# Hybrid HGRN2 / latent-attention / SwiGLU layer: tokens handed over column by column, the first weight block as an array of its own, token sums loaded one by one

## The reference

```
h    = rms_norm(x, attn_norm_w)
proj = h @ w_in                        # 2048 x 5184: hq hf hi hg (1024 each), c_q 512, c_kv 512, k_r 64
o_a  = hgrn2_mixer(hq, hf, hi, hg)     # gated linear recurrence in chunks of 64
o_b  = mla_mixer(c_q, c_kv, k_r)       # low-rank attention, RMS norms on the latents and on each head
x    = x + concat(o_a, o_b) @ w_out
h    = rms_norm(x, ffn_norm_w)
x    = x + (silu(gate) * up) @ w_down  # gate, up = h @ w_gate_up, D_FF = 5632
```

## Time and profile before

| | |
|---|---|
| median of 3 runs | 1115.05 us (1113.57 to 1115.18) |
| the profiled execution | 1115.01 us |
| its span, first to last instruction | 1113.3 us |
| PE busy | 1103.5 us (99%) |
| DVE / ACT / POOL busy | 900.2 / 644.7 / 61.0 us |
| DMA | 230.01 MB, mean 207 GB/s |
| chain that ended last | PE 91%, DVE 4%, DMA 2% |

### The profile page before, as it was taken

One profiled execution on the slowest core, in us unless ns is written; L12 is line 12 of the kernel. 1 busy time (PEld: TensorE's weight loads), 2 busy tenths in 40 slices (PEclk: granted clock), 3 DMA queues, 4 the chain that ended last, 5 costly groups with the idle time before them and its releaser, 6 DMA issues.

```text
span 1113.3 us, 15363 instructions
## 1 busy us (share of the span) xinstructions
PE 1103.5 (99%) x5176; PEld 927.6 (83%) x5176; DVE 900.2 (81%) x1234; ACT 644.7 (58%) x910; POOL 61.0 (5%) x154
## 2 busy tenths in 40 slices
PE   8999999999999999999999999999999999999998
PEld 7988888888888888888888888888888878888887
DVE  6688787587876577588988888988988889999887
ACT  7566777668654466365455555554554555655553
POOL 4200000000000000000000000000000020000000
PEclk9999999999999999999999999999999999999999
DMA  8766455554655455767777777787777786666665
GB/s 269 209 187 200 146 169 157 157 162 152 230 183 172 164 176 171 227 218 224 234 236 225 228 233 220 230 240 218 233 237 228 233 290 210 200 215 202 197 205 170
DMA packets 107557, 230.01 MB, mean 207 GB/s; under 512 B 8265, under 2 KB 19314, under 8 KB 107250
## 3 DMA queue, kind: packets, MB, share of 16 engines
q1 hardware_dynamic: 101346, 209.30, 60.3%
q0 software_dynamic: 5856, 19.93, 5.7%
q10 hardware_dynamic: 304, 0.14, 0.0%
HBM read 218.85 MB, written 10.49 MB: 206 GB/s over the span
## 4 chain that ended last, share of the span: by engine, by line
PE 91%; DVE 4%; DMA 2%; ACT 1%; issue 1%; SPq 0%; DVEq 0%; ACTq 0%
PE side L1975 22%; PE main L1731 20%; PE side L1977 11%; PE main L1734 10%; PE side L1945 4%; PE side L1946 4%; PE side L1947 4%; PE main L1945 3%; PE main L1946 3%; PE main L1947 3%; DMA raw<-in_w_down 1%; PE main L1751 1%; PE side L1773 1%; DVE w_lo L1122 1%; PE side L1870 1%
## 5 line engine op out<-in xcount | busy, mean ns | idle before, releaser
L1013 ACT CAST w_hi<-raw 128x1024 fp32r<-128x1024 f32 x245 | 239.8, 984 | 162.8 <-PE side L1975 62.8
L1573 DVE TENSOR_TENSOR w_lo<-raw,w_hi 128x1024 fp32r<-128x1024 f32 x245 | 274.6, 1133 | 17.7 <-ACT w_hi L1013 17.5
L1122 DVE TENSOR_TENSOR w_lo<-raw,w_hi 128x1024 fp32r<-128x1024 f32 (+3 forms) x156 | 178.8, 1156 | 97.1 <-ACT w_hi L793 94.4
L793 ACT CAST w_hi<-raw 128x1024 fp32r<-128x1024 f32 (+3 forms) x156 | 153.4, 993 | 130.2 <-PE main L1731 125.4
L1731 PE MATMUL main<-w_hi,hT_hi 128*128 128x512 f32 (+2 forms) x416 | 161.2, 388 | 0.2 <-issue 0.2
L1734 PE MATMUL main<-w_hi,hT_lo 128*128 128x512 f32 (+2 forms) x416 | 157.6, 380 | 0.0
L1975 PE MATMUL side<-w_hi,hT_hi 128*128 128x512 f32 x400 | 155.6, 389 | 0.0
L1977 PE MATMUL side<-w_hi,hT_lo 128*128 128x512 f32 x400 | 155.6, 389 | 0.0
L1731 PE MATMUL main<-w_lo,hT_hi 128*128 128x512 f32 (+2 forms) x416 | 107.1, 379 | 0.0
L1975 PE MATMUL side<-w_lo,hT_hi 128*128 128x512 f32 x400 | 106.9, 389 | 0.0
L1731 PEld LDWEIGHTS main<-w_hi,hT_hi 128*128 128x128 f32 x416 | 78.2, 188 | 13.2 <-issue 0.4
(11 more groups left out here) (292 smaller groups left out, 1887.5 us busy)
## 6 DMA issues: line engine op xcount, KB each, us to landing
raw<-in_w_gate_up SPq DMA_DIRECT2D x176, 512.0 KB, 4.8
raw<-in_w_down SPq DMA_DIRECT2D x88, 512.0 KB, 4.5
raw<-in_w_in SPq DMA_DIRECT2D x64, 512.0 KB, 4.0
raw<-in_w_out SPq DMA_DIRECT2D x32, 512.0 KB, 3.6
raw<-in_w_in SPq DMA_DIRECT2D x15, 384.0 KB, 5.0
squares<-hiddenT POOLq DMA_DIRECT2D x11, 512.0 KB, 5.3
hiddenT<-squares POOLq DMA_DIRECT2D x44, 128.0 KB, 5.2
raw<-in_w_ukv SPq DMA_DIRECT2D x8, 512.0 KB, 4.0
```

The lines of the kernel that those rows point to most:

```text
L793: copy(w_hi[:, slot, 0:n], raw[:, slot, 0:n]).then_inc(s_hi, 1)
L1013: copy(w_hi[:, n % RING, 0:cols], src).then_inc(s_hi, 1)
L1122: tt(w_lo[:, slot, 0:n], raw[:, slot, 0:n], w_hi[:, slot, 0:n].bitcast(F32), ALU.subtract)\
L1573: tt(w_lo[:, n % RING, 0:cols], src, w_hi[:, n % RING, 0:cols].bitcast(F32), ALU.subtract)\
```

## The change

- **x with columns on partitions.** The host hands over a second copy of x, `columns`: per partition p the 41 norm weights that belong to it, then 16 tiles of 256 tokens. The loads (`load_tokens`, nine of them) put it into `x_columns`, which lies over the memory of `hT_lo`; ACT rounds it from there into `hT_hi`, DVE writes `hT_lo` over it in place. The transposes of x and of the norm weights are gone from PE, and `vec_cols` is the start of `x_columns`, filled by the first load.
- **The first block's weights** are a contiguous array of their own, `w_first` (2048 x 384). Its first granule is loaded from ACT's queue, the others from SP's.
- **x itself** (tokens on partitions) is still needed for the squares and is loaded later, in four loads of 512 KB behind the loads of granules 11, 12, 14 and 16. `sq1` moves to positions 10, 12, 13 and 15, `r1a` and `r1b` to 16 and 17.
- **r_in** is no longer there when block 0's products are read: `lat_in` copies them unscaled, `lat_a` scales inside the square, and `lat_b` multiplies by both factors. `k_r` is still scaled in `lat_in`.
- **POOL's wait** is now for the last of these four loads; the three small loads that are left come behind granules 18 to 20.
- **Token sums** are asked for one product at a time, when PE has used 0, 0, 4, 8, 13, 19, 25, 31, 37 and 43 granules of w_down.

The core of the diff:

```
+SUMS_FROM = (0, 0, 4, 8, 13, 19, 25, 31, 37, 43)
-X_AFTER = {1: (2,), 2: (3,), 3: (4,), 4: (5,), 5: (6,), 6: (7,), 7: (8,)}
-X_TURNED = (FIRST, -1, 1, 2, 3, 4, 5, 6, 7)
+XT_AFTER = {1: (1,), 2: (2,), 3: (3, 4), 4: (5,), 5: (6,), 6: (7,), 7: (8,)}
+X_AFTER = {11: 0, 12: 1, 14: 2, 16: 3}
+SMALL_AFTER = 18
...
-    s = [(FIRST, ("vec", 0))] + [(at, ("x", p)) for p, at in enumerate(X_TURNED)]
-    s += [(2 * c + 3, ("sq1", c)) for c in range(4)]
-    s += [(10, ("r1a",)), (11, ("r1b",)), (19, ("vec", 1))]
+    s = [(at, ("sq1", c)) for c, at in enumerate((10, 12, 13, 15))]
+    s += [(16, ("r1a",)), (17, ("r1b",))]
...
+        x_columns = sb("x_columns", [P, GAP + KT * SEQ], F32, loaded)[:, GAP - V_ROWS:]
+        loaded.close()
+        sb("vec_cols", [P, GAP])
+        vec_cols = x_columns[:, 0:V_ROWS]
         hT_lo = sb("hT_lo", [P, KT, SEQ], F32R)
...
+        def load_tokens(p):
+            k, wide = PIECES[p]
+            c0, c1 = V_ROWS + SEQ * k if p else 0, V_ROWS + SEQ * (k + wide)
+            nc.sync.dma_start(x_columns[:, c0:c1], columns[:, c0:c1]).then_inc(s_xt[p], 16)
...
-            load_x(sp, 0)
-            for g, (b, k, n) in enumerate(GRANULES):
+            load_tokens(0)
+            for g in range(1, G0):
                 if g >= RING:
                     slot_free(g)
+                load_granule(sp, g)
+                for p in XT_AFTER.get(g, ()):
+                    load_tokens(p)
+                if g in X_AFTER:
+                    cols = slice(NB * X_AFTER[g], NB * (X_AFTER[g] + 1))
+                    sp.dma_start(X[:, :, cols], x_v[:, :, cols]).then_inc(s_x[X_AFTER[g]], 16)
...
-            pool.wait_ge(s_x[len(PIECES) - 1], 16)
+            pool.wait_ge(s_x[3], 16)
             pool.dma_start(lb[:, :, :], hgrn_lb[:, 0:GW].partition_broadcast(P)).then_inc(s_lbin, 16)
...
-                pool.wait_ge(s_used, W1 + 2 * c)
                 for n, p in enumerate(CHUNKS[c]):
+                    pool.wait_ge(s_used, W1 + SUMS_FROM[p])
...
                 elif kind == "sq1":
                     c = a[0]
+                    act.wait_ge(s_x[c], 16)
...
+                    act.wait_ge(s_inv, RMS.index(("r1a",)) + 1)
                     for t in range(NT):
-                        square(latents[i][:, t, :], sumsq[:, t:t + 1])
+                        square(latents[i][:, t, :], sumsq[:, t:t + 1], scale=r_in[:, t:t + 1])
...
-                        ts(v, v, inv[:, t:t + 1], None, ALU.mult).then_inc(s_lat, 1)
+                        ts(v, v, inv[:, t:t + 1], r_in[:, t:t + 1], ALU.mult, ALU.mult).then_inc(s_lat, 1)
...
-            act.dma_start(vec_rows[0:KT, :], attn_norm_w.rearrange("a (k p) -> (a k) p", p=P)).then_inc(s_attn, 16)
-            load_x(act, 1)
+            load_granule(act, 0)
```

More of the change, by code:

```diff
@@ L79, in main_blocks @@
     for n, cols in enumerate(LAT_COLS):
-        w.append(("lat", n, "w_in", at, cols, rows(KT), 2))
+        w.append(("lat", n, "w_in", at, cols, rows(KT), 2) if n else ("lat", n, "w_first", 0, cols, rows(KT), 2))
         at += cols
@@ L274, in schedule @@
     s += [(e + 3, ("r2a",)), (e + 4, ("r2b",))]
+    s += [(at, ("x", p)) for p, at in enumerate(X_SPLIT)]
     return sorted(s, key=lambda x: x[0])
@@ L359, in split_needed, with hybrid_layer @@
     return SPLIT[("x", len(PIECES) - 1)] + 1
-def hybrid_layer(nc, x, positions, attn_norm_w, w_in, hgrn_lb, hgrn_norm_w, mla_q_norm_w, w_uq, mla_kv_norm_w,
-                 w_ukv, q_head_norm_w, k_head_norm_w, w_out, ffn_norm_w, w_gate_up, w_down, out):
-    weights = {"w_in": w_in[0], "w_uq": w_uq[0], "w_ukv": w_ukv[0], "w_out": w_out[0]}
+def hybrid_layer(nc, x, columns, positions, w_first, w_in, hgrn_lb, w_uq, w_ukv, q_head_norm_w, k_head_norm_w, w_out, w_gate_up,
+                 w_down, out):
+    weights = {"w_first": w_first, "w_in": w_in[0], "w_uq": w_uq[0], "w_ukv": w_ukv[0], "w_out": w_out[0]}
     w_gu = w_gate_up[0]
@@ L494, in hybrid_layer @@
         s_tlo = sem("s_tlo")
-        s_x = [sem(f"s_x{p}") for p in range(len(PIECES))]
-        s_attn = sem("s_attn")
+        s_xt = [sem(f"s_xt{p}") for p in range(len(PIECES))]
+        s_x = [sem(f"s_x{c}") for c in range(4)]
         s_small = sem("s_small")
@@ L844, in step @@
                 kind, a = s[0], s[1:]
[L845 to L851, removed]
+                if kind == "x":
+                    k, wide = PIECES[a[0]]
+                    act.wait_ge(s_xt[a[0]], 16)
+                    split_hi([(hT_hi[:, k + n, :], x_turned(k + n), V_ATTN + k + n) for n in range(wide)])
                 elif kind == "sq1":
                     c = a[0]
-                    for p, (k, _) in enumerate(PIECES):
-                        if k // 4 == c:
-                            act.wait_ge(s_x[p], 16)
+                    act.wait_ge(s_x[c], 16)
                     for t in range(NT):
@@ L1050, in _ @@
                     convert(n % RING, loads(n), n, granule_size(n))
-                for s in split_steps_at(g):
+                for s in steps_at(g):
                     step(s)
@@ L1212, in step @@
                 if kind == "x":
-                    ps, (k, wide) = filled(s), PIECES[a[0]]
-                    split_lo(s, [(hT_lo[:, k + n, :], ps[:, n * SEQ:(n + 1) * SEQ], hT_hi[:, k + n, :],
-                                  V_ATTN + k + n) for n in range(wide)])
+                    k, wide = PIECES[a[0]]
+                    dve.wait_ge(s_thi, SPLIT[s] + 1)
+                    for n in range(k, k + wide):
+                        ins = stt(out=hT_lo[:, n, :], in0=x_turned(n), scalar=vec_cols[:, V_ATTN + n:V_ATTN + n + 1],
+                                  in1=hT_hi[:, n, :].bitcast(F32), op0=ALU.mult, op1=ALU.subtract)
+                    ins.then_inc(s_tlo, 1)
                 elif kind in ("r1a", "r2a"):
@@ L1914, in lhs_of @@
                 return (mT_hi, mT_lo, ks) if kind == "uq" else (hT_hi, hT_lo, ks)
-            for g in range(FIRST, 0):
-                for s in steps_at(g):
-                    step(s)
             for g, (b, k, n) in enumerate(GRANULES):
@@ L2068, in granule_size @@
     return n * BLOCKS[b][4]
-_INS = ["x", "positions", "attn_norm_w", "w_in", "hgrn_lb", "hgrn_norm_w", "mla_q_norm_w", "w_uq", "mla_kv_norm_w",
-        "w_ukv", "q_head_norm_w", "k_head_norm_w", "w_out", "ffn_norm_w", "w_gate_up", "w_down"]
+_INS = ["x", "columns", "positions", "w_first", "w_in", "hgrn_lb", "w_uq", "w_ukv", "q_head_norm_w", "k_head_norm_w", "w_out",
+        "w_gate_up", "w_down"]
 def kernel(**inputs):
@@ L2081 @@
     rows = np.concatenate([np.arange(P), np.arange(SEQ - 1, P - 1, -1)])
+    laid = {**inputs, "x": inputs["x"][:, rows], "positions": inputs["positions"][:, rows]}
+    norms = [inputs[f"{n}_w"][0].reshape(-1, P).T
+             for n in ("attn_norm", "ffn_norm", "mla_q_norm", "mla_kv_norm", "hgrn_norm")]
+    x_columns = laid["x"][0].T.reshape(KT, P, SEQ).transpose(1, 0, 2).reshape(P, KT * SEQ)
+    laid["columns"] = np.concatenate(norms + [x_columns], axis=1)
+    laid["w_first"] = inputs["w_in"][0][:, 4 * HG:4 * HG + LAT_COLS[0]]
     for name in _INS:
-        a = np.ascontiguousarray(inputs[name][:, rows] if name in ("x", "positions") else inputs[name])
+        a = np.ascontiguousarray(laid[name])
         arrays[f"in_{name}"] = a
```

66 lines of the change are left out of this document (24 added, 42 removed).

## The result

The change made the kernel **slower**: 1119.68 us (median of 5 runs, 1119.48 to 1121.77) against 1114.37 us for the kernel before (5 runs, 1113.41 to 1115.18). The forecast was 1109.8 us, in a range of 1108.0 to 1112.6. The profiled execution took 1119.6 us with a span of 1117.8 (before: 1115.01 and 1113.3).

The account below looks back on a forecast made before the run. PE was taken to bound the kernel, busy for 1103.5 of 1113.3 us. Block 0's 3.5, the second transpose's 0.4 and the token sums' 1.3 sum to 5.2, so 1115.0 becomes 1109.8 us, range 1108.0 to 1112.6.

Parts of the forecast that it names:

- the first one: After the first 11 us up to w_down: all runs at PE's pace, so block 0's 3.5 us gain reaches the end.
- was given back on the way: Sign of being wrong: the same total time although block 1 starts at 24.
- POOL's wait: POOL's work ends at 52 us, DVE needs it at 72.87 - 4: cover 17 us, cost nothing.
- The start: Block 0: third piece starts at 9.0 instead of 10.34; the block gains 3.5 us, 2.2 of transposes included.
- The first rival: Block 0: PE stays longer at 1.2 GHz, third piece in effect no earlier than 10.34; 1111.1 us, chance 0.2.
- The squares and x's second loading: Blocks 1 and 2: moved squares and 2.1 MB more of x fit beside the weights, needing 292 GB/s; cost nothing.
- The rival that came nearest to the measured time: Granules 13 to 17: x's second loading starves PE, which loses 7.9 us; 1117.7 us, chance 0.05 for the whole loss.
- The second transpose: Block 2: dropping the second transpose of norm weights saves 0.4 us.
- The sums: Start of w_down: token sums asked for later remove both PE stops, saving 1.3 us.
- lat_b's second factor: Scaling of lat: the extra factor replaces instructions one for one and costs nothing.
- The Trainium skill's rule that the prediction weighs: Loads of x ahead of the third piece: runs off 256-byte multiples cost one transaction more, 0.3 us less gain.

Follow-up runs that it names:

- e1: Kernel before with only vec_cols moved between hT_hi and hT_lo, so hT_lo and X start 192 bytes later: 1122.89 us, ratio 1.0075.
- e2: The change with the 192 bytes between hT_hi and hT_lo made 512: 1112.3 us, ratio 0.9976 to the kernel before.
- e14: The change with POOL's constants waiting for the last piece of x's columns, not x's second loading: 1118.05 us, ratio 1.0039 to the kernel before.
- e9: e2 with POOL's constants waiting for the last piece of x's columns, not x's second loading: 1109.39 us, ratio 0.9958 to the kernel before.
- e10: e9 with the three small loads put behind granule 22: 1109.82 us, ratio 0.9960 to the kernel before.
- e6: e5 with lat's two factors multiplied first, so lat is scaled by one factor: ratio 0.9972 to the kernel before.
- e5: e2 with the three small loads put behind granule 22 instead of 18: ratio 0.9980 to the kernel before.
- e4: The change with block 0's weights read out of w_in as before, not the contiguous w_first: 1120.31 us, ratio 1.0052 to the kernel before.
- e3: Kernel before with each load of token sums waiting until shortly before its use: 1112.88 us, ratio 0.9991.
- e7: Kernel before with junk between hT_hi and hT_lo, so hT_lo and X start 768 bytes later: 1114.14 us, ratio 0.9994.
- e13: Kernel before with vec_cols between hT_lo and X, so only X and ident start 192 bytes later: 1113.43 us, ratio 0.9993.
- e12: Kernel before with 384 bytes between hT_hi and hT_lo, so hT_lo starts 128 past a multiple of 256: 1124.97 us, ratio 1.0098.

## Why the prediction was wrong

**The step that failed** is the first one: "Everything between runs at PE's pace, so what block 0 saves is carried through to the end". I took PE's pace as given and looked for waits alone. What came is what the prediction lists as a sign of being wrong, a gain that "was given back on the way". The two lines of the diff that put `vec_cols` ahead of `hT_lo` have no term in the sum at all; they cost 0.6 us in each group of the FFN, 6 us there, and more in the blocks ahead of it (block 1 takes 17.01 us in the change and in e1, 16.63 in e2 and 16.64 before). Taken back alone (the change against e2) they are worth 7.4 us by the medians, 8.1 by the ratios. No row of the trace of before shows such a cost, since `hT_hi` and `hT_lo` were both well placed there; what could have been seen is that the diff moves an operand of some 1,050 matmuls.

**POOL's wait: "Cover 17 us; cost nothing."** The cover was measured to DVE's first use of POOL's masks. Between lies DVE's scaling of `lat`, which uses nothing of POOL's but did not run beside its MEMSETs, and PE stood for it. The 512 KB of `hgrn_lb`, which moved with the wait, are in no sum of the prediction either. Taken back alone (e14) it is worth 1.6 us by the medians, 1.1 by the ratios; the stop that went is 1.2.

**The start**, 3.5 us, was 2.6: right in kind, too large. The third piece began at 9.35, not 9.0, and its first four matmuls took 9.35 to 10.77, 0.355 us each and not 0.174; that is 0.7 us which the sum did not have. Three of the four came 0.32 us apart, which is 384 columns at 1.2 GHz, the lower of PE's two levels. The column of the granted clock reads 1.00 there, but the record of the granted clock in this trace only starts at 10.99 us. It starts at 7.87 in e2 and at 8.54 in e9, and there these four matmuls took 0.82 and 0.72 us. The first rival had named it. So the start varies between executions: with nearly the same beginning, block 1 began at 23.54 in e2, 23.86 in e9, 24.17 in e10, 24.32 in e6, 24.35 in e14, 24.37 in e5 and 24.64 in e4; 24.0 lay among them, and the change's profiled execution at their end. With the old beginning and well-placed operands it began at 26.86 to 27.68 (before, e3, e7, e13). Mean against mean of these the start is worth 3.2 us; the 2.6 has some bad luck in it.

**The squares and x's second loading**, at nothing: near enough for PE. No wait of PE for weights stands on the list of after, behind the start (e9 and e10 have one each at 33 us, 0.4 and 0.5 us, for `w_lo`); from 24 to 37 us the DMA moved 327 GB/s, over the 292 that were needed (the window's last column).

```profile
24.00:37.00 13.00, 13.00 (x76) 13.00 (x75) 6.37 (x8) 7.94 (x17) 1.11 (x2) 1.00 0.98 327
```

But the weights did come late: ACT's waits for them between 20 and 54 us grew from 1.8 to 10.2 us (after: us, times, longest), and in e5, where they are 7.6, DVE came to `lat` 1.2 us earlier than in e2, where they are 9.9.

```profile
ACT w_hi L802 <- DMA raw<-in_w_in: 10.2, 6, 2.9
```

The rival that came nearest to the measured time, 1117.7, gave it for a reason that the trace does not show: PE lost nothing to starving in block 1. Its nearness is luck.

**The second transpose**, 0.4: about right. In e9 and e10, which have no stop there, block 2's start to its first 512 columns takes 15.11 and 14.94 us against 15.31 before, so 0.2 to 0.4. **The sums**, 1.3: the profiled w_down is 1.5 shorter, the timed runs of e3 give 1.0 (0 to 2.0). **lat_b's second factor**, one for one: without POOL two scalings take 1.00 us with it and 0.88 without, 0.1 us.

With the two side effects taken out, e9 is at 1109.4 where the sum said 1109.8; the terms together were near enough, and what decided was not among them.

The Trainium skill's rule that the prediction weighs, on runs of x that start off a multiple of 256 bytes in memory, was not tried: the array's rows are 16548 bytes long in every kernel here that has it.

## What to carry to other kernels

Where a diff inserts, drops or resizes an on-chip array, work out the new start of every array behind it, and keep the stationary operands of hot matmuls on multiples of 256 bytes (shown here for fp32 tiles of 128 x 128); a busier PE with fewer matmuls and no waits is the sign of it. When a wait moves an engine's idle-time chores later, look at what runs beside them in the new place on the other engines, not only at who needs their result, and at which loads move along with them.

## What was not expected of the hardware

The start of an fp32 stationary operand costs time though nothing waits: 227 ns from one 512-column product to the next where both operands start on multiples of 256 bytes, up to 241 where `hT_lo` starts 192 past one, while the recorded weight loads of `hT_lo` keep their 188 ns (L1971 in the change, L1977 in e1; in e12 those of `hT_hi` on L1975 read 189 and 191). One operand 64, 128 or 192 bytes off costs 7.4 to 11.0 us in this kernel, and both together, at 192, less than one alone: 4.9.

A short stop can cost more than its own length. In e2's profile PE stood 2.08 us ahead of the transposes of `lat` and ran the eight of them; then, from 52.24 to 55.65, the granted clock was 0.5 (1.2 GHz), and products of 320 columns came every 0.27 us and not every 0.145. e4's profile shows the same behind a stop of 2.34 us; behind the 1.30 and 1.85 us in those of e5 and e6 the clock stayed at 1.00. Windows of e2 and then of the change, which stood 1.22 us:

```profile
51.00:53.00 2.00, 1.79 (x12) 1.82 (x13) 2.00 (x4) 1.44 (x5) 0.00 (x0) 0.81 0.61 220
53.00:55.00 2.00, 2.00 (x9) 2.00 (x9) 1.79 (x4) 0.45 (x2) 0.00 (x0) 0.50 0.92 282
```

```profile
51.00:53.00 2.00, 0.94 (x9) 0.97 (x10) 2.00 (x4) 1.32 (x2) 0.18 (x1) 1.00 0.82 251
53.00:55.00 2.00, 2.00 (x16) 2.00 (x15) 2.00 (x4) 1.31 (x5) 0.00 (x0) 1.00 0.57 111
```

Nine matmuls in 2 us against sixteen. It does not happen in every execution: a mean granted clock of 0.998 stands beside 4 of e2's 11 (1112.69 to 1113.74, the lowest of all 1109.75) and 6 of e5's 12 (1112.33 to 1115.26, lowest 1110.35). In e9, without the stop, all five read 1.000 and lie within 1.5 us.
